# A hybrid encoder step with the prompt cross attention run by pairs of heads, the first expert block taken out of its loop, and scaling work moved between engines

## What is computed

```python
def cross_attend(h, mk, mv, p):
    B, T = h.shape[:2]
    q = (h @ p['w_xq']).reshape(B, T, X_HEADS, X_HEAD_DIM)
    s = jnp.einsum('bthd,bmhd->bhtm', q, mk).astype(jnp.float32) * X_SCALE
    pr = jax.nn.softmax(s, axis=-1)
    o = jnp.einsum('bhtm,bmhd->bthd', pr.astype(mv.dtype), mv).reshape(B, T, X_WIDTH)
    return o @ p['w_xo']

def moe(h, p):
    T, D = h.shape
    logits = (h @ p['w_router']).astype(jnp.float32) + p['b_router'].astype(jnp.float32)
    top_val, top_idx = lax.top_k(logits, TOP_K)
    gate_w = jax.nn.softmax(top_val, axis=-1)
    ...
        gu = xblk @ p['w_gu'][e] + p['b_gu'][e]
        gate = jnp.minimum(gu[..., :EXPERT_FF], SWIGLU_LIMIT)
        up = jnp.clip(gu[..., EXPERT_FF:], -SWIGLU_LIMIT, SWIGLU_LIMIT)
        glu = gate * jax.nn.sigmoid(gate * SWIGLU_ALPHA)
        return ((up + 1.0) * glu) @ p['w_down'][e] + p['b_down'][e]
```

## Time and profile before

| | |
|---|---|
| runs | 1544.94, 1539.69, 1544.83 us (median 1544.83) |
| profiled execution | 1544.59 us |
| its span, first to last instruction | 1542.7 us |
| around the span | 1.9 us |
| TensorE busy | 96% of the span |
| VectorE, ScalarE, GpSimd busy | 33%, 19%, 3% |
| read from HBM | 475.18 MB |
| chain that ended last | TensorE 75%, DMA 18%, VectorE 3% |

### The profile page before, as it was taken

One profiled execution on the slowest core, in us unless ns is written; L12 is line 12 of the kernel. 1 busy time (PEld: TensorE's weight loads), 2 busy tenths in 40 slices (PEclk: granted clock), 3 DMA queues, 4 the chain that ended last, 5 costly groups with the idle time before them and its releaser, 6 DMA issues.

```text
span 1542.7 us, 20062 instructions
## 1 busy us (share of the span) xinstructions
PE 1475.9 (96%) x7661; PEld 717.5 (47%) x7662; DVE 501.8 (33%) x1234; ACT 285.5 (19%) x634; POOL 40.2 (3%) x44
## 2 busy tenths in 40 slices
PE   7999899999998989999999999999999999999995
PEld 6776577556885553333333333333333333333331
DVE  3446453003132364242232322332332322322314
ACT  1235555010012320011111110111110111111111
POOL 0100000000005200000000000000000000000000
PEclk9999999999999989999999999999999999999998
DMA  9403166732433377999999999996999999999994
GB/s 274 150 28 133 65 230 221 245 109 82 151 109 112 114 287 286 427 429 428 429 428 429 428 428 428 429 428 264 416 429 429 428 428 428 429 429 428 429 428 194
DMA packets 80489, 480.81 MB, mean 312 GB/s; under 512 B 16112, under 2 KB 44048, under 8 KB 53824
## 3 DMA queue, kind: packets, MB, share of 16 engines
q1 hardware_dynamic: 67792, 471.78, 74.9%
q0 software_dynamic: 2016, 6.49, 1.1%
q10 hardware_dynamic: 10640, 1.98, 0.7%
...
HBM read 475.18 MB, written 4.65 MB: 311 GB/s over the span
## 4 chain that ended last, share of the span: by engine, by line
PE 75%; DMA 18%; DVE 3%; ACT 1%; issue 1%; DVEq 0%; SPq 0%; ACTq 0%
PE bank L476 70%; DMA ring<-in_w_gu 18%; PE bank L1105 1%; PE bank L790 1%; PE bank L1148 1%; PE bank L490 1%; DVE small L1512 0%; PE bank L846 0%; PE bank L985 0%; PE bank L801 0%; DVE rstd L1373 0%; PE bank L728 0%; DVE rstd L1369 0%; DVE ring L1509 0%; DMA xr<-in_x_prompt 0%
## 5 line engine op out<-in xcount | busy, mean ns | idle before, releaser
L476 PE MATMUL bank<-ring,latent 128*64 128x512 f32 (+2 forms) x3328 | 739.2, 586 | 11.0 <-DMA ring<-in_w_gu 11.0
L476 PEld LDWEIGHTS bank<-ring,latent 128*64 128x64 f32 (+1 forms) x3328 | 253.2, 139 | 468.8 <-issue 431.3
L1817 DVE TENSOR_SCALAR latent<-bank 128x512 f32<-128x512 f32 x33 | 22.8, 691 | 599.7 <-PE bank L476 599.7
L1803 DVE TENSOR_TENSOR xr<-xr,bank 128x512 f32<-128x512 f32 x204 | 127.4, 678 | 39.2 <-PE bank L476 39.2
L476 PE MATMUL bank<-hT,ring 128*128 128x384 f32 x384 | 124.4, 486 | 0.0
L476 PE MATMUL bank<-ring,hT 128*128 128x256 f32 (+1 forms) x480 | 108.6, 388 | 0.0
L476 PE MATMUL bank<-latent,fkT 64*128 64x512 f32 x408 | 105.7, 623 | 0.8 <-ACT latent L2160 0.8
L2152 ACT ACTIVATE probTs<-latent 128x512 f32<-128x512 f32 x33 | 20.8, 630 | 454.0 <-DVE latent L1817 454.0
L476 PE MATMUL bank<-heads,latent 128*64 128x512 f32 x396 | 95.0, 616 | 5.2 <-DVE latent L1698 5.2
L476 PEld LDWEIGHTS bank<-ring,hT 128*128 128x128 f32 x480 | 92.2, 193 | 15.3 <-issue 0.9
L476 PEld LDWEIGHTS bank<-hT,ring 128*128 128x128 f32 x384 | 72.9, 190 | 50.2 <-issue 0.2
...
## 6 DMA issues: line engine op xcount, KB each, us to landing
ring<-in_w_gu SPq DMA_DIRECT2D x128, 2048.0 KB, 19.8
...
```

The costliest lines, as they stand in the source:

```text
L476: return pe.matmul(o, l, r, start=start, stop=stop, skip_group_check=True)
L1803: v.tensor_tensor(x, x, banks[i][:, :], ALU.add).then_inc(shares_added, 1)
L1817: v.tensor_scalar(gS, gate[:, :], LIMIT, None, ALU.min).then_inc(gate_clipped, 1)
```

## The change

The prompt's units are paired the other way: two token tiles of the same two heads. TensorE makes three queries, then the scores of the first pair (heads 0 and 1), the fourth query, the first cache's turning, and so on, so that the steps of pair, cache and samples alternate; `mem_scores(0)` moves ahead of the second pair's turning. VectorE's and ScalarE's lists follow. `normal_rows` goes from VectorE to ScalarE. The first expert block's down part leaves the loop: behind `gate_and_up(0)` stand the gathering of block 1, the tables, `turn_hidden(0)` and `down(0, 0)`; the loop runs one round fewer, and its shares of zeros go. At the end VectorE multiplies the first tile by the gain ahead of the root, one root serves all three tiles, ScalarE scales the first tile last, and GpSimd does nothing there.

```diff
@@ -440,7 +441,7 @@
                 return [("fox", t, hs) for t in range(2) for hs in ((0, 2), (1, 3), (4, 6), (5, 7))]
             if kind == "mla":
                 return [("mla", t, (g, g + 4)) for t in range(2) for g in range(4)]
-            return [("mem", t, (2 * g, 2 * g + 1)) for t in range(2) for g in range(2)]
+            return [("mem", t, (2 * g, 2 * g + 1)) for g in range(2) for t in range(2)]
...
@@ -970,11 +971,12 @@
             for t in range(NT):
                 for half in range(2):
                     pe.wait_ge(free(("xT", t, half)), count(("xT", t, half)))
-            for j in range(2):
-                s = arrived(pe, ("xq", j))
-                for m in range(2):
-                    i = project_T(("xq", 2 * j + m), s, P * m, hT)
-                used_last(pe, i, ("xq", j))
+            def cross_queries(h):
+                s = arrived(pe, ("xq", h // 2))
+                i = project_T(("xq", h), s, P * (h % 2), hT)
+                used_last(pe, i, ("xq", h // 2))
...
@@ -1016,16 +1018,30 @@
                 used_last(pe, i, ("cm", b))
-            mem_turn(0)
-            for h in range(XH):
+            first, second = XUNITS[0:2], XUNITS[2:4]
+            for h in range(3):
+                cross_queries(h)
+            for h in range(2):
                 pe.wait_ge(free(("xq", h)), count(("xq", h)))
                 pe.wait_ge(free(("mkT", h)), count(("mkT", h)))
+            scores(U_MEM, first)
+            cross_queries(3)
+            mem_turn(0)
+            for m in range(2):
+                turn(U_MEM + m, first[m])
+            for h in range(2, XH):
+                pe.wait_ge(free(("xq", h)), count(("xq", h)))
+                pe.wait_ge(free(("mkT", h)), count(("mkT", h)))
+            scores(U_MEM + 2, second)
+            mem_turn(1)
             for t in range(2):
                 for j in range(2):
                     pe.wait_ge(free(("xv", t, j)), count(("xv", t, j)))
-            pipeline(XUNITS, U_MEM, lambda j: mem_turn(1) if j == 0 else None)
-            for u in range(NXU):
-                pe.wait_ge(free(("V", U_MEM + u)), count(("V", U_MEM + u)))
+            values(U_MEM, first)
+            mem_scores(0)
+            for m in range(2):
+                turn(U_MEM + 2 + m, second[m])
+            values(U_MEM + 2, second)
...
             for b in range(NB + 2):
-                if b < NB:
+                if 0 < b < NB:
                     mem_scores(b)
                 if 1 <= b <= NB:
                     mem_probs(b - 1)
@@ -1056,6 +1072,9 @@
                     turn_back(("cO", b - 2), mem_rows[b % 2], ("cV", b - 2))
                 if 1 < b + 1 < NB:
                     mem_turn(b + 1)
+                if b == 2:
+                    for u in range(NXU):
+                        pe.wait_ge(free(("V", U_MEM + u)), count(("V", U_MEM + u)))
                 if b in CROSS_AT:
                     cross_out(*CROSS_AT[b])
...
+            def finish(a, more):
+                pe.wait_ge(y_copied, a + 1)
+                if more:
+                    pe.wait_ge(member_ready, a + 3)
+                    take_rows()
+                start_down()
+                pe.wait_ge(share_ready, a + 1)
+                add_shares(0)
+                pe.wait_ge(gate_clipped, a + 2)
+                add_shares(1)
+                if more:
+                    pe.wait_ge(rows_copied, a + 3)
+                    turn_rows()
+                turn_hidden(a + 1)
+                pe.wait_ge(up_clipped, a + 2)
+                pe.wait_ge(shares_added, a * 6 + 1)
+                add_shares(2)
+                down(a + 1, pe.value_load(block_turn[0:1, bass.ds(a + 1, 1)], min_val=0, max_val=NE - 1))
...
@@ -1170,6 +1201,9 @@
             turn_rows()
             pe.wait_ge(xT_ready, 1)
             gate_and_up(0)
+            pe.wait_ge(member_ready, 2)
+            take_rows()
+            start_down()
             pe.wait_ge(picks_ready, 1)
...
+            pe.wait_ge(rows_copied, 2)
+            turn_rows()
             pe.wait_ge(cols_ready, 1)
             for j in range(4):
                 i = mm(tables_bank[:, 64 * j:64 * j + 64], bc(table_cols[:, j:j + 1], [P, P]), ident[:, 0:64], j == 0, j == 3)
             i.then_inc(owners_ready, 1)
+            turn_hidden(0)
+            down(0, 0)
             pe.wait_ge(counts_ready, 1)
-            last_blk = pe.value_load(blocks_i[0:1, 0:1], min_val=NE - 1, max_val=NBLK - 1)
+            later = pe.value_load(blocks_i[0:1, 0:1], min_val=NE - 2, max_val=NBLK - 2)
             pe.wait_ge(tables_ready, 1)
-            with pe.Fori(0, last_blk) as b:
-                turn = pe.value_load(block_turn[0:1, bass.ds(b, 1)], min_val=0, max_val=NE - 1)
-                finish(b, turn, True)
-                turn = pe.value_load(block_turn[0:1, bass.ds(b + 1, 1)], min_val=0, max_val=NE - 1)
-                pe.wait_ge(xT_ready, b + 2)
-                pe.wait_ge(shares_added, b * 6 + 6)
+            turn = pe.value_load(block_turn[0:1, 1:2], min_val=0, max_val=NE - 1)
+            pe.wait_ge(xT_ready, 2)
+            gate_and_up(turn)
+            with pe.Fori(0, later) as a:
+                finish(a, True)
+                turn = pe.value_load(block_turn[0:1, bass.ds(a + 2, 1)], min_val=0, max_val=NE - 1)
+                pe.wait_ge(xT_ready, a + 3)
+                pe.wait_ge(shares_added, a * 6 + 6)
                 gate_and_up(turn)
...
@@ -1313,10 +1352,6 @@
                 pool.wait_ge(bias_step, 5 * c + 5)
                 pool.dma_start(bias3[64:96, o], bmid).then_inc(bias_moved, 16)
                 pool.wait_ge(bias_moved, 32 * c + 32)
-            pool.wait_ge(gfin_loaded, 16)
-            pool.wait_ge(first_scaled, 1)
-            nc.gpsimd.tensor_tensor(yout[:, 0, :], yout[:, 0, :], gfin, ALU.mult).then_inc(fin_ready[0], 1)
...
@@ -1639,8 +1672,18 @@
                 give(v.tensor_tensor(o, o, ps[:, :], ALU.add), ("xo", t, j))
+            for u in range(2):
+                part1(U_MEM + u, XUNITS[u])
+            for u in range(2):
+                part2(U_MEM + u, XUNITS[u])
+            dve.wait_ge(free(("xq", 3)), count(("xq", 3)))
+            v.tensor_copy(xpair[:, :, :, 0:NQ], xqT[:, :, 256:384].rearrange("p h (b q) -> p b h q", q=NQ)).then_inc(pairs_ready, 1)
             mem_out(0)
-            pipeline(XUNITS, U_MEM, lambda j: mem_out(1) if j == 0 else None)
+            for u in range(2, 4):
+                part1(U_MEM + u, XUNITS[u])
+            mem_out(1)
+            for u in range(2, 4):
+                part2(U_MEM + u, XUNITS[u])
...
             scale_turned("rT", 1, gf_c, hT)
             dve.wait_ge(square_sum, n0 + 2)
             inverse_root(rstd[:, n0:n0 + 2], ssq[:, n0:n0 + 2], D)
-            def normal_rows(t):
-                v.tensor_scalar(xn2[:, t, :], xr[:, t, :], rstd[:, n0 + t:n0 + t + 1], None, ALU.mult).then_inc(xn_ready, 1)
+            v.nop().then_inc(router_root, 1)
...
@@ -1767,6 +1807,14 @@
             link(v.tensor_copy(inblk, row_i))
             link(v.tensor_copy(blkf, blk_i))
             link(v.tensor_scalar(inblk, inblk, 1.0, None, ALU.add))
+            dve.wait_ge(seats_added, 1)
+            find_members(slice(1, 2))
+            dve.wait_ge(places_known, 1)
+            dve.wait_ge(member_ready, 1)
+            list_seats()
+            dve.wait_ge(rows_full, 1)
+            dve.wait_ge(seats_added, 2)
+            mark_members()
...
+            def weigh(b, second):
+                v.tensor_scalar(share, token, owners[:, b], owners[:, second], ALU.is_equal, ALU.mult).then_inc(share_ready, 1)
+            activate(0)
+            dve.wait_ge(owners_ready, 1)
+            v.tensor_copy(tables_i, tables_bank[0:1, 0:256])
+            link(v.tensor_copy(bexp, tables_bank[:, 64:64 + NBLK + 1]))
+            v.tensor_copy(owners[:, 0:114], tables_bank[:, 256:370]).then_inc(tables_ready, 1)
+            xT_out(2, slice(1, 2))
+            dve.wait_ge(tables_ready, 1)
+            weigh(slice(0, 1), slice(NBLK + 1, NBLK + 2))
...
             dve.wait_ge(gfin_loaded, 16)
+            dve.wait_ge(shares_added, later * 6 + 8)
+            v.tensor_tensor(yout[:, 0, :], xr[:, 0, :], gfin, ALU.mult).then_inc(first_scaled, 1)
             n0 = 3 * NT + 2
-            dve.wait_ge(square_sum, n0 + 1)
-            inverse_root(rstd[:, n0:n0 + 1], ssq[:, n0:n0 + 1], D)
+            dve.wait_ge(square_sum, n0 + NT)
+            inverse_root(rstd[:, n0:n0 + NT], ssq[:, n0:n0 + NT], D)
             v.nop().then_inc(root_ready, 1)
-            dve.wait_ge(square_sum, n0 + NT)
-            inverse_root(rstd[:, n0 + 1:n0 + NT], ssq[:, n0 + 1:n0 + NT], D)
...
+            for u in range(2):
+                exps(U_MEM + u, XUNITS[u])
+            copy_out(("xq", 3), xqT[:, 3, :], TOK)
             mem_out(0)
-            pipeline(XUNITS, U_MEM, lambda j: mem_out(1) if j == 0 else None)
+            for u in range(2):
+                probs_out(U_MEM + u, XUNITS[u])
```

(20 more changed lines are left out.)

106 lines of the change are left out of this document (41 added, 65 removed).

## The result

| | before | after |
|---|---|---|
| median of six runs each, us | 1544.68 | 1528.63 |
| lowest to highest, us | 1539.69 to 1547.61 | 1527.76 to 1533.48 |
| profiled execution, us | 1544.59 | 1527.76 |
| its span, us | 1542.7 | 1525.6 |

The ratio is 0.9903, 95% interval 0.9885 to 0.9921: the change makes the kernel 16 us, about 1%, faster. The forecast was 1525.7 in a range of 1518.5 to 1534.

What follows compares the result with a forecast made beforehand. The expert-weight stream was taken to bound the kernel, so the end follows from when it runs without pause. Savings of 8.0 (cross attention), 0.7 (router), 7.6 (first block) and 2.6 (end), 18.9 in all, took 1544.59 to 1525.7; range 1518.5 to 1534.

Steps and rivals of the forecast that it cites:

- First block, -7.6: Expert block 0, end of gate/up to first slots back: 12.0 us instead of 19.6; bounds 6.5 and 8.2.
- Cross attention, -8.0: Prompt's cross attention: reordered work covers 3.8 us of TensorE's waits, the rest from the clock; bounds 2 and 10.
- The step on the clock: Cross attention: without the idle stretch, values (5.56 us) run in half, 2.8 back, plus 1.4 for a later low stretch.
- Router, -0.7: Router: VectorE's three scalings (2.07 us) leave the path, but the ranks let only 0.7 us through; bounds 0 and 0.9.
- Loop, 0: Expert loop: a table load between shares and down part stays covered; uncovered 0.5 us a block.
- End, -2.6: Final norm: last add to VectorE's first output product takes 3.6 us instead of 6.2; bounds 2.0 and 2.8.
- The stream, 0: Expert weights after block 0: the stream, its hole and the last block move as a whole, nothing lost.
- The signs: Trace marks named beforehand: loads near 593, VectorE waits under 2, no low clock around 500, same hole, root steps under 0.3.
- Rival 1: Cross attention: VectorE and GpSimd block each other elsewhere, saving 3.2 us instead of 8; 1530.5, chance 0.13.
- Rival 2: Weight stream does not follow: half of the first block's 7.6 us goes into a longer hole; 1529.5, chance 0.05.
- Rival 3: Samples' loop: TensorE's clock stays low throughout, costing 28 us and making the kernel slower; 1553.5, chance 0.03.
- Rival 4: Cross attention: in-order VectorE and ScalarE put the wait elsewhere, only the other parts' 10.9 us come; 1533.7, chance 0.05.

Runs made afterwards that it cites:

- after_again: The changed kernel, unedited, profiled and measured once more: 1529.7 us, ratio 0.9893.
- hold_bias: The changed kernel with GpSimd's second and third piece of bias work held until the prompt's cross attention values are out: 1526.56 us, ratio 0.9878.
- cross_alone: The kernel before the change with only the new order of the prompt's cross attention: 1539.53 against 1545.78 us, ratio 0.9959.

## Why the prediction was right, and where its terms were not

The sum against the first profile, before and after, from the table: start +0.2; first query to the end of `gate_and_up(0)` -8.9; to `w_down(1)` -7.9; to the last wait +0.8; the end -1.3: together -17.1 (1542.7 to 1525.6). The forecast was -18.9, the medians say -16.1. Two misses, 1.3 at the end and 0.8 in the stream, are most of the difference. What bounds the kernel was read rightly: the stream's start moved by 609.53 - 592.93 = 16.6 and nearly all of that came out at the end.

- **First block, -7.6: right.** -7.9 against the kernel before, in every run that has it. The pause went from 9.7 to 1.7 us; worked out were 8.8 and 1.2.
- **Cross attention, -8.0: right in kind, but it has no single value.** The first profile gives -9.2, the waits left are 3.6 of the 4.2 forecast. But the same code gave -5.4 to -5.9 in five other executions: the mean of all eight is 42.7, so -7.0. The step on the clock was wrong twice. I halved the whole 5.56 us of the values as if all of it had run at the lower level. At the upper level the same products take 1.95 + 2.02, and at the lower one half of them alone takes 3.75 (after_again): only part of the 5.56 was slow, and 1.6 came back there, not 2.8. That the clock's share was still 4.2 in sum is luck. All of TensorE's waits fell from 8.6 to 3.6, which leaves 4.2 of the 9.2, and another 1.1 of it lies in the turnings of probabilities (0.65 + 0.66 + 2.25 before, 1.04 + 1.46 after), which the sum had not named. And I took the clock for a consequence of the pause, when behind one and the same pause it falls or does not.
- **Router, -0.7: right**, 0.5 to 0.6.
- **Loop, 0: right.** SyncE's groups of `w_gu` follow each other at TensorE's pace by 28.1 to 28.2 us in both traces (645.14 to 673.28, 628.53 to 656.68).
- **End, -2.6: the term that failed.** VectorE's first output product does come 2.6 earlier, and the end only 1.3. The step "so 2.6 less" costed the engine's steps and left out the three writes behind them, 3.9 us at their rate, which before had been issued over 3.1 us (1536.47 to 1539.59) and now over 1.4.
- **The stream, 0: 0.8 lost.** The stretch from `w_down(1)` to the last wait is 900.2 and 900.3 with the old first block, 900.5 to 901.4 with the new. SyncE's queue shows where it goes. `w_down(10)` is issued 253.45 behind `w_down(1)` in both kernels, `w_down(11)` 281.67 behind it before and 282.53 after; from there they follow by 29.4 in both, and over the hole by 57.51 in both. So the hole is as long as before, and the 0.8 is one step, at the place where TensorE catches up with the stream: its first wait for a load comes 268 behind `w_down(1)` after and 297 before, one expert sooner. The bytes moved are the same (426 GB/s over the 240 us behind `w_down(1)` in both). Why TensorE catches up sooner, and whether it has to do with the shorter pause, no run tells. Two lines before, two after:

```profile
862.98 3.77 SPq L1224 DMA_DIRECT2D ring<-in_w_down  x2
891.20 3.77 SPq L1224 DMA_DIRECT2D ring<-in_w_down  x2
846.38 3.77 SPq L1263 DMA_DIRECT2D ring<-in_w_down  x2
875.46 3.77 SPq L1263 DMA_DIRECT2D ring<-in_w_down  x2
```

**The signs.** The last loads at 593, the wait for VectorE's product under 2 (1.49), no root step above 0.17 and the hole came as named. No low clock around 500 held in the first profile and not in after_again (0.68 between 490 and 506), so it was a sign that one execution can show by chance.

**Rivals.** Rival 1 is true as a mechanism: VectorE and GpSimd meet at just the place named, in all eight executions (the small scaling takes 1.49 to 1.89), and hold_bias prices it at 1.6 to 2.0 us with the clock up, 5 to 5.6 with the clock down behind it. In the five executions with the lower clock the cross attention saved 5.4 to 5.9, between the forecast's 8.0 and this rival's 3.2. At 0.13 it stood too low; its time, 1530.5, is 2 us from the median. It did not undo the forecast because what it left in the first profile, 3.6 of waits, is what the forecast had left for softmax latency. Rival 2 fell: it put half of 7.6 into a longer hole, and the hole is as long as before, with 0.8 lost ahead of it. Rival 3's mechanism exists on a smaller scale: after_again and hold_bias have low clock at the end of the samples' loop behind a pause, at a cost of 3 and 5 us, not 28 (its 1553.5 should read 1553.7: 1525.7 + 28). Rival 4 fell with cross_alone.
